# Norm transposes made as products with a diagonal, weight splits moved, and norm steps reordered, in a fused two-block transformer kernel

## What is computed

```python
def rmsnorm(x, g):
    xf = x.astype(jnp.float32)
    y = xf * lax.rsqrt(jnp.mean(xf * xf, axis=-1, keepdims=True) + EPS)
    return (y * g.astype(jnp.float32)).astype(x.dtype)

for i in range(DEPTH):
    u = rmsnorm(x, norm_pre[i])
    y = mixer(u, ...)              # ends in  o @ w_out
    x = x + rmsnorm(y, norm_post[i])

def conv_ffn(x, w_up, conv_w, conv_b, w_down):
    h = x @ w_up                   # [512, 5632]
    h = causal_conv3(h, conv_w) + conv_b
    a, u = jnp.split(h, 2, axis=-1)
    return (jax.nn.gelu(a, approximate=True) * u) @ w_down
```

## Time and profile before

| what | value |
|---|---|
| time of 3 runs, us | 2292.16 (2289.88 to 2293.75) |
| the profiled execution's own time, us | 2292.16 |
| its span, us | 2290.2 |
| PE busy | 2077.7 us (91%) |
| PEld busy | 1669.0 us (73%) |
| DVE, ACT, POOL busy, us | 845.6, 934.7, 915.5 |
| mean granted TensorE clock | 0.931 of full speed |

### The profile page before, as it was taken

How to read it: one execution, slowest core, us unless ns; L and a number is a source line. 1 busy time by engine, 2 the same in 40 slices (tenths; PEclk the granted TensorE clock), 3 DMA queues, 4 the chain that set the end, 5 groups by cost and what they waited for, 6 DMA issues and landing times.

```text
span 2290.2 us, 33582 instructions
## 1 busy us (share of the span) xinstructions
PE 2077.7 (91%) x13582; PEld 1669.0 (73%) x13582; DVE 845.6 (37%) x1813; ACT 934.7 (41%) x1707; POOL 915.5 (40%) x636
## 2 busy tenths in 40 slices
PE   4999899989997978996688989999989898999998
PEld 3889766778865745875566678887878577888787
DVE  2100467330027465157565353333033435343301
ACT  3431377453346444442132354343243545444322
POOL 2431267534456322341013624544434542445442
PEclk9996999999998979898598999999999999999999
DMA  3322100123310211222110313332322112333322
GB/s 118 93 77 65 56 11 2 56 67 96 94 50 23 66 47 52 77 64 47 43 31 15 109 57 102 92 98 96 108 70 82 55 56 62 97 99 92 102 101 83
DMA packets 222360, 161.03 MB, mean 70 GB/s; under 512 B 30631, under 2 KB 205295, under 8 KB 222208
## 3 DMA queue, kind: packets, MB, share of 16 engines
q1 hardware_dynamic: 220016, 151.83, 22.4%
q0 software_dynamic: 2192, 7.07, 1.0%
HBM read 153.64 MB, written 5.24 MB: 69 GB/s over the span
## 4 chain that ended last, share of the span: by engine, by line
PE 81%; DVE 8%; ACT 4%; issue 3%; POOL 2%; DMA 1%; POOLq 1%; SPq 0%; DVEq 0%; PEld 0%; PEldq 0%; ACTq 0%
PE ps L380 15%; PE ps L347 13%; PE ps L348 13%; PE ps L353 13%; PE ps L390 8%; PE ps L1341 2%; PE ps L1354 2%; PE ps L1330 2%; POOL weights_lo L289 1%; PE ps L2877 1%; ACT buffer L648 1%; PE ps L1068 1%; ACT weights_hi L278 1%; PE ps L2890 1%; PE ps L2119 1%
## 5 line engine op out<-in xcount | busy, mean ns | idle before, releaser
L289 POOL TENSOR_TENSOR weights_lo<-buffer,weights_hi 128x1024 fp32r<-128x1024 f32 (+1 forms) x265 | 654.2, 2471 | 1001.7 <-ACT weights_hi L278 1001.4
L278 ACT ACTIVATE weights_hi<-buffer 128x1024 fp32r<-128x1024 f32 (+1 forms) x265 | 276.3, 1045 | 356.1 <-PE ps L390 299.6
L347 PE MATMUL ps<-u_hi,weights_hi 128*128 128x512 f32 (+1 forms) x752 | 282.6, 380 | 6.7 <-DVE u_lo L675 6.3
L348 PE MATMUL ps<-u_lo,weights_hi 128*128 128x512 f32 (+1 forms) x752 | 281.9, 379 | 0.0
L1916 ACT ACTIVATE buffer<-ps,buffer 128x512 f32<-128x512 f32 x88 | 68.7, 780 | 278.3 <-PE ps L353 278.3
L353 PE MATMUL ps<-u_hi,weights_lo 128*128 128x512 f32 (+1 forms) x752 | 176.8, 378 | 0.0
L1947 DVE SCALAR_TENSOR_TENSOR buffer<-ps,buffer,buffer 128x511 f32<-128x511 f32 x88 | 66.0, 750 | 287.7 <-ACT buffer L1916 287.7
L347 PEld LDWEIGHTS ps<-u_hi,weights_hi 128*128 128x128 f32 x752 | 143.7, 191 | 33.3 <-DVE u_lo L675 6.9
L348 PEld LDWEIGHTS ps<-u_lo,weights_hi 128*128 128x128 f32 x752 | 143.9, 191 | 25.3
L353 PEld LDWEIGHTS ps<-u_hi,weights_lo 128*128 128x128 f32 x752 | 136.8, 191 | 25.7
L380 PE MATMUL ps<-weights_hi,act_hi 128*128 128x512 f32 x352 | 110.8, 397 | 10.7 <-POOL weights_lo L289 10.2
(11 more groups left out here) (397 smaller groups left out, 4265.9 us busy)
## 6 DMA issues: line engine op xcount, KB each, us to landing
buffer<-in_w_up SPq DMA_DIRECT2D x88, 512.0 KB, 3.8
buffer<-in_w_down SPq DMA_DIRECT2D x44, 512.0 KB, 3.4
buffer<-in_diff_w_in SPq DMA_DIRECT2D x32, 512.0 KB, 4.0
buffer<-in_nsa_w_in SPq DMA_DIRECT2D x28, 512.0 KB, 3.8
buffer<-in_w_rkv SPq DMA_DIRECT2D x24, 512.0 KB, 3.9
buffer<-in_nsa_w_out SPq DMA_DIRECT2D x8, 512.0 KB, 3.6
buffer<-in_diff_w_out SPq DMA_DIRECT2D x8, 512.0 KB, 3.7
buffer<-in_w_o_rwkv SPq DMA_DIRECT2D x8, 512.0 KB, 3.5
```

The lines of the kernel that those rows point to most:

```text
L278: self.nc.scalar.activation(self.part_hi[:, part % self.PARTS, 0:n], self.raw[:, ld % self.RAW, 0:n], ACT.Copy).then_inc(self.hi_ready, 1)
L289: self.nc.gpsimd.tensor_tensor(self.part_lo[:, part % self.PARTS, 0:n], self.raw[:, ld % self.RAW, 0:n], self.part_hi[:, part % self.PARTS ...
L347: nc.tensor.matmul(out, hi[:, k, :], rhs[0][:, k, tokens], start=(k == 0), stop=False)
L348: nc.tensor.matmul(out, hi[:, k, :], rhs[1][:, k, tokens], start=False, stop=False)
```

## The change

It has six parts.

1. `unit` no longer scales the row tile. It scales the 128x128 identity by the rows' inverse roots into one of two small buffers, and `turn` multiplies the unscaled rows with that diagonal, an ordinary float32 product instead of a transpose. From tile 2 on ACT waits until the buffer's last use is over.
2. ACT's order in `Output`: `unit(1)` stands ahead of `square(3)`, and `high(1)` right behind `square(3)`, ahead of the next split and of `square_x(2)`.
3. DVE's order: `low(0)` as before behind `invert(1)`; `low(1)` now inside the last `add`, ahead of the addition to x.
4. The first product ahead starts with the high activation parts alone, and waits only for those (and for the bank that it writes); the products with the low parts follow behind a wait of their own.
5. `FfnUp`: the high parts of the second and third `w_down` loads are made in the last load's turn and ahead of `gelu(21)`, not behind `act_hi(20)` and `act_hi(21)`.
6. `DiffAttend` makes the parts of its two loads at u = 12 and u = 22, `SwaAttend` those of its three at u = 11, 19 and 27, on ACT and POOL alike.

```diff
@@ project_features
+def project_features(..., between=None, lows=None):
         nc.tensor.matmul(out, hi[:, k, :], rhs[0][:, k, tokens], start=(k == 0), stop=False)
-        nc.tensor.matmul(out, hi[:, k, :], rhs[1][:, k, tokens], start=False, stop=False)
+        if not lows:
+            nc.tensor.matmul(out, hi[:, k, :], rhs[1][:, k, tokens], start=False, stop=False)
+    if lows:
+        lows()
+        for k in range(KD):
+            nc.tensor.matmul(out, hi[:, k, :], rhs[1][:, k, tokens], start=False, stop=False)
@@ Renorm
     def unit(self, act, i):
         act.wait_ge(self.env.rstd_ready, self.n + i + 1)
-        self.env.nc.scalar.activation(self.un[:, i, :], (self.env.x if self.g_row is None else self.un)[:, i, :], ACT.Copy,
+        if i >= 2:
+            act.wait_ge(self.env.un_turned, self.n + i - 1)
+        self.env.nc.scalar.activation(self.unit_of(i), self.env.ident, ACT.Copy,
                                       scale=self.rstd[:, i:i + 1]).then_inc(self.env.un_ready, 1)
+    def unit_of(self, i):
+        return self.env.lambda_work[:, (i % 2) * P:(i % 2 + 1) * P]
@@ turn
-            out, rows = env.ps[:, 2 * i + k // 4, (k % 4) * P:(k % 4 + 1) * P], self.un[:, i, k * P:(k + 1) * P]
-            tr = nc.tensor.transpose(out, rows, env.ident)
+            out = env.ps[:, 2 * i + k // 4, (k % 4) * P:(k % 4 + 1) * P]
+            rows = (env.x if self.g_row is None else self.un)[:, i, k * P:(k + 1) * P]
+            tr = nc.tensor.matmul(out, rows, self.unit_of(i), start=True, stop=True)
+    def wait_high(self, pe, tiles):
+        pe.wait_ge(self.env.uhi_ready, self.hi_n + tiles)
@@ Output.tensor
             if self.ahead:
-                self.norm.wait(pe, 2)
+                self.norm.wait_high(pe, 2)
+                self.norm.wait(pe, 1 + self.ahead[0][1] % 4 // 2)
             for i in range(2, NT):
                 for ld, g in self.ahead[i - 2:i - 1]:
-                    project_features(env, pe, ld, self.norm.u, g, tokens=EARLY)
+                    project_features(env, pe, ld, self.norm.u, g, tokens=EARLY,
+                                     lows=(lambda: self.norm.wait(pe, 2)) if i == 2 else None)
@@ Output.scalar
             self.norm.high(act, 0)
+            self.norm.unit(act, 1)
         square(3)
         if self.norm:
-            self.norm.unit(act, 1)
+            self.norm.high(act, 1)
             env.split_hi(act, self.lds[-1] + 1)
             square_x(2)
-            self.norm.high(act, 1)
             self.norm.unit(act, 2)
@@ Output.vector
                                            ALU.mult).then_inc(env.proj_taken, 2)
+            if self.norm and i == NT - 1:
+                self.norm.low(dve, 1)
...
-                if i >= 2:
-                    self.norm.low(dve, i - 2)
+                if i == 2:
+                    self.norm.low(dve, 0)
@@ DiffAttend; SwaAttend has SPLITS = [11, 19, 27] and self.ahead - 2
+    SPLITS = [12, 22]
-            if u == 8:
-                env.split_hi(act, self.ahead)
+            if u in self.SPLITS:
+                env.split_hi(act, self.ahead - 1 + self.SPLITS.index(u))
-            if u == 8:
-                self.env.split_lo(pool, self.ahead)
+            if u in self.SPLITS:
+                self.env.split_lo(pool, self.ahead - 1 + self.SPLITS.index(u))
@@ FfnUp.scalar
-                env.split_hi(act, self.lds[n] + 1)
+                env.split_hi(act, self.lds[n] + (2 if n == 2 * FT - 1 else 1))
...
+        env.split_hi(act, self.lds[-1] + 3)
         gelu(FT - 1)
         act_hi(FT - 2)
-        env.split_hi(act, self.lds[-1] + 2)
         act_hi(FT - 1)
-        env.split_hi(act, self.lds[-1] + 3)
```

More of the change, by code:

```diff
@@ L331, in w_cols, with project_features @@
     return w.rearrange("(k p) m -> p k m", p=P)[:, :, c0:c0 + n]
-def project_features(env, pe, ld, rhs, g, cols=P, ready=None, tokens=slice(0, T), bank=None, between=None):
+def project_features(env, pe, ld, rhs, g, cols=P, ready=None, tokens=slice(0, T), bank=None, between=None, lows=None):
     nc = env.nc
@@ L2109, in width @@
         return P * (1 + (self.pairs[u][1] > 0))
+    SPLITS = [11, 19, 27]
     HALVES = [slice(0, 64), slice(64, 128)]
@@ L2190, in scalar @@
         for u in range(n_pairs + self.AHEAD):
-            if u == 8:
-                env.split_hi(act, self.ahead)
+            if u in self.SPLITS:
+                env.split_hi(act, self.ahead - 2 + self.SPLITS.index(u))
             if 2 <= u < n_pairs:
@@ L2222, in gpsimd @@
         for u in range(n_pairs + 2):
-            if u == 8:
-                self.env.split_lo(pool, self.ahead)
+            if u in self.SPLITS:
+                self.env.split_lo(pool, self.ahead - 2 + self.SPLITS.index(u))
             if u < n_pairs:
```

## The result

The changed kernel takes 2279.72 us (median of 7 runs, 2272.59 to 2283.73) against 2292.04 (7 runs, 2289.43 to 2293.75). The ratio is 0.9947, with a 95% interval of 0.9933 to 0.9961: faster by 12 us, where 34 were forecast. The profiled execution took 2276.2 us.

What follows compares the result with a forecast made beforehand. PE was taken to bound the kernel, busy 2077.7 of 2290.2 us, with gaps also lowering its clock. Terms 14.5 + 14.9 + 1.9 + 3.1 + 0 - 0.6 = 33.8 took 2292.2 to 2258.5 us; range 2247 to 2275.

Steps and rivals of the forecast that it cites:

- Products for transposes: Turns in five `Output` stages: eight products take 1.06 us against 1.03 for transposes, costing 0.6 us over 20 tiles.
- Feed-forward ends: Both `w_down` ends: earlier high parts close PE's 5.08 us gap and save low clock, gaining 14.5 us together.
- The four handovers: Stage handovers with products ahead: reordering, shorter `unit` and early high products gain 14.9 us, between 11.8 and 18.8.
- Diff to RWKV: From diff to RWKV: shorter `unit(2)`, `unit(3)` and earlier `high(1)` gain 1.9 us, between 1.5 and 2.4.
- First norm: In `Norm`: four shorter units on ACT's chain, less a limit passing to DVE's `gain`, gain 3.1 us.
- the last rival: `unit` and `turn` wait for each other's buffers; said to cost nothing, as that turn is always done; chance 0.01.
- The attentions: Moved splits in swa and diff: 0 us overall, between a gain of 4 and a loss of 8.
- Float32 products cost what transposes don't: Rival for the turns: three more of 1.03 us for each of 24, 74 us, giving 2333; chance 0.02.
- The clock stays up: Rival at the handovers: shorter gaps keep PE's clock high, gaining 18.8 rather than 14.9, about 2252 us; chance 0.14.
- The attentions lose more: Rival: each of five moved splits lowers the clock and the pipeline fills slowly, 10 us more, about 2269; chance 0.12.
- the wait for `unit`: Sign of being right: PE's idle time at `turn` for `unit` falls from 2.57 to under 1 us.
- turns of more than 1.3 us at full clock: Sign of being wrong: turns by products last over 1.3 us, where eight products were read as 1.06.

Runs made afterwards that it cites:

- e5: Kernel before with part 1 alone (products for transposes, small `unit`): 2296.62 us against 2290.89, ratio 1.0042.
- e3: Changed kernel with part 1 undone (`unit` and `turn` put back, transposes again), moved splits kept: 2274.69 us, ratio 0.993 to the kernel before.
- e1: Kernel before with part 5 alone (second and third `w_down` splits earlier): 2275.25 us against 2290.89, ratio 0.9939.
- e4: Kernel before with parts 2 to 5 alone, transposes and both attentions' splits at u = 8 as before: 2270.55 us, ratio 0.9912.
- e12: Kernel before with parts 2, 3 and 5 and transposes, without part 4: 2269.52 us, ratio 0.9916 to the kernel before.
- e10: Kernel before with parts 2 to 5, plus swa's high parts at u = 9, 17, 25 and low parts at 11, 19, 27: 2264.44 us, ratio 0.988.
- e14: Changed kernel with only swa's high parts moved to u = 9, 17, 25: 2268.19 us, ratio 0.9906 to the kernel before.
- e2: Changed kernel with swa's three splits back at u = 8: 2277.26 us against 2291.62 for the kernel before, ratio 0.9935.
- e16: Kernel before with parts 2 to 5 and swa's high parts at u = 9, 17, 25, the same kernel as e10 run again: 2263.51 us, ratio 0.9885.
- e9: Kernel before with every transpose of a turn issued twice, `unit` as before: 2307.98 us against 2291.62, ratio 1.0076.

## Why the prediction was wrong, and where it was right

- **Products for transposes: the step that failed.** The working took the earlier trace rows for "eight products 1.06 us". The row's x8 counts instructions, and eight of them are four products. A turn of eight products has 16 and takes 1.95 us at full clock, not 1.06. With 0.92 us more for each of the 20 turns that the working counts, the term is 18.4 us instead of 0.6, and the sum gives 2276.3 instead of 2258.5. That is an upper price, since not every turn is on the path: the traces charge 11.0 us in the handovers and 1.7 from diff to RWKV (both below), 12.7 of the 21.2 us by which the forecast missed, more than any other term. e5 bears it out: alone, part 1 costs 6 to 10 us where the forecast had a gain in it. Taking it out of the change (e3) gives 4 to 5. It could have been seen beforehand: `values` at line 1712 makes one product for each of up to four tiles, so a group of eight is more than one unit issues.
- **Feed-forward ends, 14.5 forecast: right.** 14.1 in the change and in e1. The order of events was as worked out.
- **The four handovers, 14.9 forecast: 3.9.** The orders are worth 10.1 with transposes. A `unit` of 0.3 us instead of 1.13 was to bring up to 4 x 0.83 = 3.3 of the 14.9, so some 11.6 was forecast for the orders alone; they brought 1.5 us less, within their ends. With the measured 0.40 us the short `unit` gives 4 x 0.73 = 2.9. The products take 0.92 more in each of three turns, four times, 11.0. 10.1 + 2.9 - 11.0 = 2.0, where 3.9 was measured; the 1.9 us left over fit the 10 us less of low clock than in e4, but no run isolates them. From nsa to diff the first product ahead starts 4.67 us behind the last line 390 (now 396) instead of 7.06: 2.4 us sooner where 3 were forecast, with a `turn(1)` that lasts 2.05 us instead of the 1.1 counted on. That the early high products need no low part (part 4) was right, and is worth the 0.77 us of e12's row in three handovers.
- **Diff to RWKV, 1.9 forecast: -0.7.** The orders bring -0.4 (e4). Against e4, PE's waits for the two short units are 1.7 us shorter, but `turn(2)`, at the low clock, takes 3.56 us instead of 1.97 and `turn(3)` 2.05 instead of 1.97, 1.7 in all.
- **First norm, 3.1 forecast: 2.4.** `unit` takes 0.40 us, not 0.3, so four save 3.0; ACT's first unit starts 0.45 us later in this trace, and the third waits 0.2 us for `turn(0)` to release its buffer, which the last rival had said would never happen. The last turn is no longer than before (1.95 us; 1.97 for eight transposes there).
- **The attentions, 0 forecast between +4 and -8: -4.4.** Diff gained 2.1. In swa POOL's wait was sized at about 1 us, that of ACT's copy alone; it was 2.2 to 2.5, because ACT comes to the copy later in its own order than POOL to the low part. So the gaps were over 3 us, not 2.2, and each lowered the clock (about 13.7 us of low clock in the stage, 10 before). Three gaps in place of one of 7.50 were forecast; their length was not. e10 and e14 show the cause.
- **Stages that the change does not touch, counted at 0:** +2.5, -5.5 and +2.1 us. Such stages scatter by more than most terms of the sum (5.1 us in nsa between the change and e2, 6.6 in the RWKV projections between e10 and e16), and a range for a clock that falls this often should hold it: 5 us or so on top of the terms' ends. The -5.5 repeats in four profiles of four of the changed code; the prediction had no term for it, and its cause is open.
- **The range.** The slow ends of all terms add up to 12.5 + 11.8 + 1.5 + 3.1 - 8 - 2 = 18.9, which is 2273, not the 2268 that stands as the terms' own end. The measured 2279.72 lies outside either, and outside 2275.
- **The rivals.** "Float32 products cost what transposes don't" named the cause with a small chance and the wrong size, 3.1 us for a turn; 0.92 was measured. The Trainium skill, TensorE: Matmul & The Clock Gate, section Terms, calls transpose mode "4× faster for FP32"; here a product of 128x128 takes twice a transpose's time, neither the same, as the prediction read its row, nor four times. "The clock stays up" came true in part: it still falls in the first three handovers of the change, for 3.5 us each instead of 7 to 10, and in the last one it stayed up in three of five profiles. That did not give the 2252 of this rival, since the turns cost more. The same page, section Part 4: PE-mode transpose, has it that a transpose does not count as busy PE "the same way"; no run here separates the two, since wherever products stand for transposes the waits of PE differ as well. "The attentions lose more" happened in swa alone. Of the signs listed, the feed-forward and the wait for `unit` (0.47 us from nsa to diff, 14.7 in all instead of 29.3) were right, and the first product ahead is released by ACT's split, but 2.4 us sooner and not 3. The gaps in swa are over 3 us where about 2 were listed, and "turns of more than 1.3 us at full clock", listed as wrong, came true.

What stays open: how much of the 1.5 us that the orders fell short is scatter of the clock's places, what decides these places from one execution to the next, and what in the change makes the RWKV projections 5.5 us longer.

## What to carry to other kernels

Count what an instruction group in a trace is made of before its duration is used as a price: a group of eight may be four operations of the program, and the code says which. Where a transpose is replaced by a float32 product, PE's time for it doubles; that pays only where the scaled copy that it saves is on the critical path by more than that, as in the first norm (2.4 us in the trace; no total shows it). When long work of one engine is cut up and spread through a pipeline, its input should be made a step or two before it is needed, or each piece brings its own wait and the sum is worse than the one long stall.

## What the runs showed of the hardware

- A float32 product of 128x128 by 128x128 is issued as two weight loads and two matmuls; sixteen take 1.95 us at full clock, much as sixteen transposes do (1.91 in e9). The weight loads of products are listed at 192 ns each in the median, those of transposes at 142, and this did not show in the turns' time.
- ACT's scaled copy of 128x128 takes 0.40 us, so the slope between 128x512 and 128x1024 does not reach down to it.
- The same RWKV projections took 172.4 to 180.0 us in five profiles, with a mean clock of 0.85 to 0.89; twice with the same kernel it was 179.97 and 179.99, and with another kernel 179.00 and 172.40. (The fifth is the kernel before, 174.50.)
- The nsa stage, without any change to it, took 2.5 us less than before in the change's profile and 2.6 us more in e2's, with the same code in both. One profile each can't tell a change of 2 us in such a stage.
